# Weight halves interleaved element by element: a stationary operand read at a step of 8 bytes

## The chip, the cores and the metric

The kernel runs on one core of a Trainium2 chip. The metric is the device time of one execution in microseconds (us), first instruction to last and the little that lies around it; lower is better.

## What is computed

One inference step of a two-layer diffusion trunk for 128 context tokens and 512 latent tokens, D = 1024. Each layer is a mixer followed by a convolutional feed-forward block of width 2816. Layer 0's mixer is a bidirectional state-space scan beside a gated convolution, layer 1's is neighbourhood attention. Cut to the products with the large weights, which take nearly all of the time:

```python
u = h @ P['ssd_w_in'][e]                                  # layer 0: 1024 -> 5664 columns
... = jnp.concatenate([y_a, y_b], -1) @ P['mix0_w_out'][e]  # 2048 -> 1024
q, k, v = split(h @ P['na_w_qkv'][o])                     # layer 1: 1024 -> 3072
... = y @ P['na_w_out'][o]                                # 1024 -> 1024
g = dwconv(h @ P['ffn_w_gate'][i], P['ffn_conv_w'][i])    # both layers: 1024 -> 2816
u = h @ P['ffn_w_up'][i]
return (jax.nn.gelu(g) * u) @ P['ffn_w_down'][i]          # 2816 -> 1024
```

The scale, shift and gate vectors come from `silu(c) @ ada_w[i]` with 6 x 1024 columns a layer. All is float32, and the outputs are the two token blocks, the scan states and the context keys and values.

## The kernel before

The activations lie transposed: features on the 128 partitions, 642 columns (128 context tokens, 2 columns of padding, 512 latent tokens) on the free axis. Every large product is cut into 244 **slots**. A slot is a column block of a weight matrix, 128 output features wide and up to 1024 input features deep: [128 partitions, 8 x 128 elements]. Every product is made in three parts for precision: the weight and the activation are each split into a rounded high part and a low rest (type float32r), and the kernel sums high x high, high weight x low activation, and low weight x high activation.

A slot goes through four engines:

- **SyncE** (`weights`, the DMA at line 366) loads the slot into one of two `raw` buffers (RAW = 2). Before it issues the load it waits until GpSimd has finished with the slot two before (`low_split`). SyncE issues everything in order, so what is queued behind a weight load waits with it. In the mixer stage that includes a 1 MB load of `ada_w` (`ada_load`, line 422) after each of the steps of a head pair.
- **ScalarE** (`split`, line 1127) copies `raw` into the high part `w_hi`, once TensorE has used the slot four before (`slot_used`; RING = 4).
- **GpSimd** (`low`, line 560) writes the low part, `w_lo = raw - w_hi`, and counts `low_split`.
- **TensorE** (`half_slot`, lines 614 to 632) waits for `low_split` and makes for each of the 8 (in the down projection 6 or 5) blocks of 128 input features six matmuls: for both halves of the columns (322 and 320) the high part with the high (line 625) and with the low activation (line 626), then the low part with the high activation for both halves (line 629). Each of the six loads its stationary operand, 128 x 128, anew. That makes 10752 matmuls of 244 slots.

`w_hi` and `w_lo` are two buffers of [128, 4, 1024] elements, each contiguous in a partition. Nothing else reads or writes them, save at the start: `first5`, one of six buffers for the first columns of `ada_w`, lies over slots 2 and 3 of `w_lo` until the low parts need the place.

VectorE and ScalarE do the rest (scaling, convolution, gelu, residuals, norms) from PSUM. `ada_step` (line 696) is the TensorE work on a loaded piece of `ada_w`; there are four in each of the 8 head pairs, and one `ada` buffer.

Of the kernel before, what the change touches and what calls it, by code (L numbers as in the profile page):

```python
# [17 lines left out]
F32 = mybir.dt.float32  # L18
F32R = mybir.dt.float32r
# [4 lines left out]
P = 128  # L24
D = 1024
C = D // P
# [26 lines left out]
RAW, RING = 2, 4  # L53
# [9 lines left out]
ADA_N = 512  # L63
# [68 lines left out]
def trunk(nc, x_prompt, x_sample, state_ssd, cache_k, cache_v, c, c_ctx, ada_w, ada_b, norm_mix_g, norm_ffn_g,  # L132
# [6 lines left out]
    with ExitStack() as ctx:  # L139
        def sb(name, shape, dt=F32):  # L140
            return ctx.enter_context(nc.sbuf_tensor(name, shape, dt))
# [3 lines left out]


        raw = sb("raw", [P, RAW, C * P])
        w_hi = sb("w_hi", [P, RING, C * P], F32R)
        first_lo_at = -(-nc.sbuf_base // 32) * 32
        w_lo = sb("w_lo", [P, RING, C * P], F32R)  # L150
        assert nc.sbuf_base == first_lo_at + RING * C * P * 4, (nc.sbuf_base, first_lo_at)
        act_hi = sb("act_hi", [P, C * T], F32R)
        outs_at = -(-nc.sbuf_base // 32) * 32
        act_lo = sb("act_lo", [P, C * T], F32R)
# [26 lines left out]
        def at(name, off, shape, dt=F32):  # L181

            n = 4
            for s in shape[1:]:
                n *= s
            assert off + n <= arena_bytes, (name, off + n, arena_bytes)
            return nc.alloc_sbuf_tensor_at(name, shape, dt, offset=at_base + off)
# [27 lines left out]
        first_at = [2 * CT, AFTER + 4 * ROW, AFTER + 4 * ROW + 8192, AFTER + 4 * ROW + 16384,  # L215
                    (arena_bytes - 2 * D * 4) // 32 * 32]
        first = [at(f"first{n}", o, [P, 4, ADA_N]) for n, o in enumerate(first_at)]
        first += [nc.alloc_sbuf_tensor_at("first5", [P, 4, ADA_N], F32, offset=first_lo_at + 2 * C * P * 4)]
        quarters = [f[:, 2 * q:2 * q + 2, :] for f in first for q in range(2)]


# [2002 lines left out]
```

## Time and profile before

| | us |
|---|---|
| median of 3 runs | 1928.59 |
| range of the runs | 1928.18 to 1929.63 |
| span of the profiled execution | 1928.4 |
| TensorE matmul busy | 1878.8 |
| TensorE weight load busy | 1797.8 |
| VectorE / ScalarE / GpSimd busy | 1025.6 / 670.9 / 637.5 |

A row of the page or of a grouping view reads: line, engine, operation, output tile <- input tiles, shape, xcount, then busy time and mean duration in ns, then the idle time of the engine before these instructions and what ended it. PE is TensorE's matmuls, PEld its loads of stationary operands, DVE VectorE, ACT ScalarE, POOL GpSimd, SPq SyncE's queue. Matmuls are pipelined: a matmul row lasts some 310 ns, though the next starts much sooner. A timeline row gives start in us, duration in us, and the instruction.

### The profile page before, as it was taken

How to read it: one execution, taken by the hardware profiler on the slowest of the kernel's cores; microseconds unless marked ns; L12 is line 12 of the kernel's file. 1: busy time of each engine (PE TensorE's matmuls, PEld its weight loads, DVE VectorE, ACT ScalarE, POOL GpSimd, SP SyncE). 2: the span in 40 equal slices, each digit the busy share in tenths (PEclk: the TensorE clock that was granted, in tenths of full speed). 3: DMA queues.
4: the chain of work that ended last, by engine and by line, in shares of the span. 5: the costliest groups of instructions: out<-in, count | busy, mean ns of one | idle time of the engine just before them, and what ended most of it. 6: DMA issues, size and time to landing. Idle time of an engine off the chain costs nothing.

```text
span 1928.4 us, 35126 instructions
## 1 busy us (share of the span) xinstructions
PE 1878.8 (97%) x13424; PEld 1797.8 (93%) x13424; DVE 1025.6 (53%) x1927; ACT 670.9 (35%) x1022; POOL 637.5 (33%) x309
## 2 busy tenths in 40 slices
PE   5999999999999999999999999999999999999997
PEld 3998888888899999999999999987899999999997
DVE  5747788877614655314554353557566553145543
ACT  4443333232413443312334321157444433123332
POOL 1223222222232323443335433433133234433341
PEclk9999999999999999999999999999999999999998
DMA  8334545445442222222222433211312222222122
GB/s 307 95 84 157 164 141 170 153 155 169 156 151 77 77 76 71 66 82 76 76 59 62 152 92 88 82 46 30 104 57 77 76 70 67 82 77 76 55 67 75
DMA packets 276232, 192.49 MB, mean 100 GB/s; under 512 B 25515, under 2 KB 259367, under 8 KB 275639
## 3 DMA queue, kind: packets, MB, share of 16 engines
q1 hardware_dynamic: 270982, 182.78, 31.1%
q10 hardware_dynamic: 5168, 8.58, 1.3%
q8 instruction: 57, 0.93, 0.2%
q14 instruction: 25, 0.20, 0.0%
HBM read 181.29 MB, written 10.04 MB: 99 GB/s over the span
## 4 chain that ended last, share of the span: by engine, by line
PE 89%; issue 5%; DVE 2%; ACT 2%; POOL 1%; DMA 1%; SPq 0%; POOLq 0%; ACTq 0%; DVEq 0%
PE ps L625 26%; PE ps L626 26%; PE ps L629 25%; PE ps L696 2%; POOL w_lo L560 1%; PE ps L1074 1%; PE ps L888 1%; PE ps L1054 1%; PE ps L1020 1%; DVE act_lo L1643 1%; ACT sp L1436 1%; PE ps L720 1%; PE ps L1093 0%; PE ps L873 0%; PE ps L808 0%
## 5 line engine op out<-in xcount | busy, mean ns | idle before, releaser
L560 POOL TENSOR_TENSOR w_lo<-raw,w_hi 128x1024 fp32r<-128x1024 f32 x244 | 601.4, 2467 | 1203.3 <-ACT w_hi L1127 1197.2
L625 PE MATMUL ps<-act_hi,w_hi 128*128 128x322 f32 x2752 | 847.5, 315 | 3.7 <-DVE act_lo L1643 2.2
L626 PE MATMUL ps<-act_lo,w_hi 128*128 128x322 f32 x2624 | 799.7, 312 | 0.0
L629 PE MATMUL ps<-act_hi,w_lo 128*128 128x322 f32 x2752 | 631.8, 311 | 0.0
L625 PEld LDWEIGHTS ps<-act_hi,w_hi 128*128 128x128 f32 x2752 | 522.0, 190 | 17.0 <-issue 13.7
L626 PEld LDWEIGHTS ps<-act_lo,w_hi 128*128 128x128 f32 x2624 | 497.7, 190 | 0.0
L629 PEld LDWEIGHTS ps<-act_hi,w_lo 128*128 128x128 f32 x2752 | 466.1, 189 | 0.0
L1127 ACT ACTIVATE w_hi<-raw 128x1024 fp32r<-128x1024 f32 x244 | 256.2, 1051 | 361.5 <-PE ps L629 321.9
L625 PE MATMUL ps<-f_hi,w_hi 128*128 128x322 f32 x704 | 213.6, 311 | 0.0
L626 PE MATMUL ps<-f_lo,w_hi 128*128 128x322 f32 x704 | 212.9, 310 | 0.0
L1958 DVE SCALAR_TENSOR_TENSOR x<-ps,mod,x 128x128 f32 (+1 forms) x96 | 48.4, 546 | 270.0 <-PE ps L629 269.4
L629 PE MATMUL ps<-f_hi,w_lo 128*128 128x322 f32 x704 | 161.0, 310 | 0.0
L626 PEld LDWEIGHTS ps<-f_lo,w_hi 128*128 128x128 f32 x704 | 133.0, 189 | 0.0
L625 PEld LDWEIGHTS ps<-f_hi,w_hi 128*128 128x128 f32 x704 | 132.9, 189 | 0.0
L1727 DVE SCALAR_TENSOR_TENSOR ft<-fg,par,ft 128x642 f32<-128x642 f32 x44 | 123.9, 2816 | 6.8 <-DVE ft L1726 6.5
L629 PEld LDWEIGHTS ps<-f_hi,w_lo 128*128 128x128 f32 x704 | 118.5, 189 | 0.0
L1995 DVE TENSOR_TENSOR fg<-ps,spread 128x642 f32<-128x642 f32 x44 | 36.3, 826 | 132.2 <-PE ps L629 122.0
L1392 ACT ACTIVATE fe<-ft,gb 128x129 f32<-128x129 f32 x88 | 44.9, 558 | 126.9 <-DVE ft L1727 126.9
L1388 ACT ACTIVATE ft<-fg,par 128x642 f32<-128x642 f32 x44 | 36.7, 834 | 127.0 <-DVE fg L1995 126.9
L1545 DVE TENSOR_TENSOR acc<-acc,sq 128x642 f32<-128x642 f32 x40 | 60.3, 1509 | 25.2 <-ACT sq L1138 25.2
L1726 DVE SCALAR_TENSOR_TENSOR ft<-fg,par,ft 128x642 f32<-128x642 f32 x44 | 43.2, 983 | 44.0 <-ACT ft L1388 43.5
L1396 ACT ACTIVATE f_hi<-fa 128x642 f32 x44 | 32.6, 742 | 94.9 <-DVE fa L2007 94.9
(297 smaller groups left out, 1932.0 us busy)
## 6 DMA issues: line engine op xcount, KB each, us to landing
ada<-in_ada_w SPq DMA_DIRECT2D x40, 1024.0 KB, 6.1
raw<-in_ssd_w_in SPq DMA_DIRECT2D x44, 512.0 KB, 4.0
raw<-in_ffn_w_gate SPq DMA_DIRECT2D x44, 512.0 KB, 3.8
raw<-in_ffn_w_up SPq DMA_DIRECT2D x44, 512.0 KB, 3.8
raw<-in_ffn_w_down SPq DMA_DIRECT2D x32, 384.0 KB, 3.4
raw<-in_na_w_qkv SPq DMA_DIRECT2D x24, 512.0 KB, 3.8
raw<-in_ffn_w_down SPq DMA_DIRECT2D x32, 320.0 KB, 3.2
first<-in_ada_w SPq DMA_DIRECT2D x16, 512.0 KB, 10.2
```

Source lines behind the costliest of these rows:

```text
L560: g.tensor_tensor(w_lo[:, s], raw[:, s % RAW], w_hi[:, s], ALU.subtract).then_inc(S["low_split"], 1)
L625: t.matmul(out, hi, chunk_of(src_hi, k0 + k, cols), start=start, stop=False)
L626: t.matmul(out, hi, chunk_of(src_lo, k0 + k, cols), start=False, stop=False)
L629: mm = t.matmul(half_out(2 * tset, h), lo, chunk_of(src_hi, k0 + k, cols), start=False, stop=stop)
L696: mm = t.matmul(ps[g:g + ADA_COLS, bank, :], csil_w[:, 2 * q + k, :], ada[:, k, b * ADA_N:b * ADA_N + ADA_N], start=(q == 0), stop=(q == A ...
L1127: a(w_hi[:, s], raw[:, s % RAW], ACT.Copy).then_inc(S["high_split"], 1)
L1388: a(ft[k][:], fg[k][:, 1:T + 1], ACT.Copy, scale=w1).then_inc(S["ffn_mid"], 1)
L1392: ins = a(fe[k][:, lo:hi], ft[k][:, lo:hi], ACT.Gelu_apprx_tanh, bias=gb[:, k, stream:stream + 1])
L1545: tt(acc[:], acc[:], sq[:], ALU.add).then_inc(S["squares_used"], 1)
L1726: st.then_wait(stt(dst[:], buf[:, 0:T], w[:, bass.ds(w0, 1)], dst[:], ALU.mult, ALU.add))
L1727: return stt(dst[:], buf[:, 2:T + 2], w[:, bass.ds(w2, 1)], dst[:], ALU.mult, ALU.add)
L1958: ins = stt(dst, V(k)[:, lo:hi], gate, dst, ALU.mult, ALU.add)
```

## The change

The two buffers become one, `w_parts` of [128, 4, 1024, 2] elements. `w_hi` is its elements 0, 2, 4, ... and `w_lo` its elements 1, 3, 5, ... in each slot. The total size is the same. ScalarE now writes `w_hi` at a step of 8 bytes. GpSimd reads `w_hi` and writes `w_lo` at a step of 8 bytes, and still reads `raw` contiguously. TensorE loads all its stationary operands in `half_slot` at a step of 8 bytes, 128 elements over 1024 bytes of a partition instead of 512. The moving operands, the PSUM outputs, the DMAs, all waits and the order of instructions stay.

`first5` moves to slot 3 of the new buffer, so it lies over both parts of slot 3 and no longer over the low parts of slots 2 and 3.

```diff
         raw = sb("raw", [P, RAW, C * P])
-        w_hi = sb("w_hi", [P, RING, C * P], F32R)
-        first_lo_at = -(-nc.sbuf_base // 32) * 32
-        w_lo = sb("w_lo", [P, RING, C * P], F32R)
-        assert nc.sbuf_base == first_lo_at + RING * C * P * 4, (nc.sbuf_base, first_lo_at)
+        w_at = -(-nc.sbuf_base // 32) * 32
+        w_parts = sb("w_parts", [P, RING, C * P, 2], F32R)
+        w_hi, w_lo = w_parts[:, :, :, 0], w_parts[:, :, :, 1]
+        assert nc.sbuf_base == w_at + RING * C * P * 8, (nc.sbuf_base, w_at)
...
-        first += [nc.alloc_sbuf_tensor_at("first5", [P, 4, ADA_N], F32, offset=first_lo_at + 2 * C * P * 4)]
+        first += [nc.alloc_sbuf_tensor_at("first5", [P, 4, ADA_N], F32, offset=w_at + (RING - 1) * C * P * 8)]
```

## Rows read from the trace of the kernel before

**Rows 1.** The page: span, and busy time of the engines with their instructions.

```profile
span 1928.4 us, 35126 instructions
PE 1878.8 (97%) x13424; PEld 1797.8 (93%) x13424; DVE 1025.6 (53%) x1927; ACT 670.9 (35%) x1022; POOL 637.5 (33%) x309
```

**Rows 2.** The page: the chain that ended last, by engine and by line.

```profile
PE 89%; issue 5%; DVE 2%; ACT 2%; POOL 1%; DMA 1%; SPq 0%; POOLq 0%; ACTq 0%; DVEq 0%
PE ps L625 26%; PE ps L626 26%; PE ps L629 25%; PE ps L696 2%; POOL w_lo L560 1%; PE ps L1074 1%; PE ps L888 1%; PE ps L1054 1%; PE ps L1020 1%; DVE act_lo L1643 1%; ACT sp L1436 1%; PE ps L720 1%; PE ps L1093 0%; PE ps L873 0%; PE ps L808 0%
```

**Rows 3.** Stretches: span, busy PE, PEld, DVE, ACT, POOL, clock, DMA share, GB/s.

```profile
32.00:36.00 4.00, 3.55 (x16) 2.74 (x20) 3.04 (x6) 2.98 (x6) 0.00 (x0) 0.50 1.07 368
38.00:40.00 2.00, 2.00 (x22) 1.38 (x15) 1.24 (x2) 1.61 (x2) 0.31 (x1) 1.00 0.44 124
800.00:1000.00 200.00, 200.00 (x1352) 200.00 (x1352) 71.92 (x93) 53.65 (x65) 75.03 (x32) 1.00 0.26 76
```

**Rows 4.** Matmuls in order of time near 34 us, wide (128-column) stationary operands.

```profile
34.03 0.47 PE L625 MATMUL ps<-act_hi,w_hi 128*128 128x322 f32 x1
34.30 0.47 PE L626 MATMUL ps<-act_lo,w_hi 128*128 128x322 f32 x1
```

**Rows 5.** The same near 39 us: 32-column operands (L752, L753), then 128-column ones.

```profile
39.02 0.31 PE L752 MATMUL ps<-act_hi,wdt_hi 128*32 128x320 f32 x1
39.16 0.31 PE L753 MATMUL ps<-act_lo,wdt_hi 128*32 128x320 f32 x1
39.46 0.31 PE L625 MATMUL ps<-act_hi,w_hi 128*128 128x322 f32 x1
39.61 0.30 PE L626 MATMUL ps<-act_lo,w_hi 128*128 128x322 f32 x1
```

**Rows 6.** Loads of 32 and of 128 columns: durations in ns, minimum, median, maximum.

```profile
L752 PEld LDWEIGHTS ps<-act_hi,wdt_hi x16: 106/108/169, 32.4 to 53.4; 128*32 128x32 f32 x16
L856 PEld LDWEIGHTS ps<-xdw,btok x48: 187/192/192, 162.1 to 455.6; 128*128 128x128 f32 x48
L625 PEld LDWEIGHTS ps<-act_hi,w_hi x2752: 186/188/334, 33.8 to 1837.2; 128*128 128x128 f32 x197
```

**Rows 7.** Six matmuls with few moving columns, merged, and the duration of one.

```profile
330.19 0.83 PE L856 MATMUL ps<-xdw,btok 128*128 128x128 f32 x6
L856 PE MATMUL ps<-xdw,btok x48: 270/275/275, 162.2 to 455.7; 128*128 128x128 f32 x48
```

**Rows 8.** The two splitting operations, grouped, and GpSimd's durations.

```profile
L560 POOL TENSOR_TENSOR w_lo<-raw,w_hi 128x1024 fp32r<-128x1024 f32 x244 | 601.4, 2467 | 1203.3 <-ACT w_hi L1127 1197.2
L1127 ACT ACTIVATE w_hi<-raw 128x1024 fp32r<-128x1024 f32 x244 | 256.2, 1051 | 361.5 <-PE ps L629 321.9
L560 POOL TENSOR_TENSOR w_lo<-raw,w_hi x244: 2343/2397/3685, 27.9 to 1895.2; 128x1024 fp32r<-128x1024 f32 x122
```

**Rows 9.** GpSimd on an access pattern in short runs, grouped.

```profile
L589 POOL TENSOR_TENSOR bias<-win,masks 128x256 f32<-128x256 f32 x48 | 33.4, 730 | 55.9 <-DVE nmax L2103 55.9
```

**Rows 10.** One slot's low part and the first matmul on it, in order of time.

```profile
1031.39 2.54 POOL L560 TENSOR_TENSOR w_lo<-raw,w_hi 128x1024 fp32r<-128x1024 f32 x1 [5.03 <-ACT w_hi L1127]
1039.78 0.31 PE L625 MATMUL ps<-f_hi,w_hi 128*128 128x322 f32 x1
```

**Rows 11.** A head pair: low part, weight load, ada load, and ada's use.

```profile
243.90 2.41 POOL L560 TENSOR_TENSOR w_lo<-raw,w_hi 128x1024 fp32r<-128x1024 f32 x1 [9.12 <-ACT w_hi L1127]
246.47 0.37 SPq L366 DMA_DIRECT2D raw<-in_ssd_w_in  x1
247.09 0.38 SPq L422 DMA_DIRECT2D ada<-in_ada_w  x1
254.28 1.06 PE L696 MATMUL ps<-ada,csil_w 128*32 128x512 f32 x8
ada<-in_ada_w SPq DMA_DIRECT2D x40, 1024.0 KB, 6.1
```

**Rows 12.** A VectorE operation with two SBUF inputs that runs beside GpSimd's.

```profile
L1727 DVE SCALAR_TENSOR_TENSOR ft<-fg,par,ft 128x642 f32<-128x642 f32 x44 | 123.9, 2816 | 6.8 <-DVE ft L1726 6.5
```

## What the change does to the time: a prediction

> **What bounds the kernel now.** The first view is the page. TensorE's matmuls are busy 1878.8 of 1928.4 us, so it sits idle for 49.6 us in all; the other engines are busy about half the span or less [rows 1]. The chain that ended last agrees: 89% of it is TensorE, and 77% are the three lines of `half_slot` [rows 2]. A busy matmul row says little about pace, because rows overlap. So the second view counts: in the 200 us from 800 to 1000, all feed-forward matmuls, 1352 start [rows 3]. That is 200 / 1352 = 148 ns from one start to the next. The change touches the stationary operand of 10752 of these, and every nanosecond on that spacing is 10.8 us. What sets the spacing is therefore the question.
>
> Three things could: the moving columns, the load of the stationary operand, or a wait. Rows 4 and 5 separate them. Near 34 us the granted clock is 0.50, the 1.2 GHz level, and the spacing is 0.27 us, which is 322 columns at 1.2 GHz (268 ns) [rows 3, 4]. Near 39 us the clock is 1.00, and with 128-column operands the spacing is 0.15 us (39.46 to 39.61) [rows 3, 5]. The matmuls just before them, with stationary operands of only 32 columns, are spaced 0.14 us (39.02 to 39.16) [rows 5]. Loading a quarter of the columns buys next to nothing, so the moving side sets the pace (322 columns at 2.4 GHz are 134 ns, and about 14 ns come on top that do not depend on the load). The loads run beside.
>
> How far beside: a load of 32 columns takes 108 ns, one of 128 takes 188 to 192 [rows 6]. That is (190 - 108) / 96 = 0.85 ns a column, so 128 columns stream in 109 ns and some 80 ns are latency. Where moving columns are few, the loads set the pace, and it shows: six matmuls with 128 moving columns take 0.83 us, less one duration of 0.275 that is 0.555 for five spacings, 111 ns each [rows 7]. So contiguous loads need 111 ns a matmul and have 148. They can grow by a third, 37 ns or 0.29 ns a column, before the time moves at all. Beyond that it moves one for one.
>
> **The change part by part.** Nothing is added, removed or reordered. Three instructions get another access pattern.
>
> *The stationary loads* (10752 on lines 625, 626, 629). No row shows a load at a step of 8 bytes. From above, a load spans twice the bytes, so I bound it by twice the streaming: 111 becomes 222 ns, the spacing 222, and 74 ns x 10752 = 796 us. From below it is nothing: no gain is possible, since even a quarter of the columns did not shorten the spacing. I take nothing, and choose it by a rate. The moving operand is read contiguously at 2.4 GHz: 322 columns of 4 bytes in 148 ns are 8.7 bytes a ns and partition, 9.6 inside its 134 ns. The stationary operand reads an element every 0.85 ns, and at a step of 8 bytes it passes over 9.4 bytes a ns. If memory hands out whole pieces of 8 or 16 bytes, the new load asks for no more pieces a ns than the moving operand already gets [rows 3, 6]. The cover is the 37 ns; without it each nanosecond of load costs 10.8 us.
>
> The Trainium skill has two statements on this, and they differ. "SBUF — State Buffer" (Door 1, the note on cachelines) says that SBUF delivers at full rate if each 16-byte line is hit at least twice; at 8 bytes a step each line is hit exactly twice, and the sum would be zero. "Vector Engine (DVE) Microarchitecture Reference" (section 5.2, the access granule) says that a VectorE port needs pairs of adjacent words, and that hopping with every element raised 1.054 to 1.73 ns a column. No run here shows either.
>
> *ScalarE's write of `w_hi`* (244 x 1051 ns) and *GpSimd's `w_lo`* (244 x 2467 ns) [rows 8]. Neither is busy enough to bind: GpSimd sat 1203 us waiting, 1197 of them for the high part, and the high part waited 322 us for TensorE to free a slot [rows 8]. A slot lasts 48 x 148 ns = 7.1 us; the two operations in series take 3.5. Bounds: ScalarE between 0 and a doubling, +1.05 us. GpSimd's nearest row with a broken pattern is 730 ns for 256 elements, 2.85 ns each against 2.41, so +0.45 us for 1024 [rows 8, 9]; its longest instance now, 3685 ns, sets the far end, +1.2 us. Call the sum of both e: 0 to 2.3 us, and I take 0.5, the GpSimd row alone. Below 0 I exclude: half as many adjacent elements cannot be quicker to write.
>
> What hides e is the ring. TensorE starts a slot well after its low part is ready: 1031.39 + 2.54 = 1033.93 against 1039.78, a slack of 5.9 us, the smallest I found once the first slots are through [rows 10]. The thinner cover is SyncE's queue. In a head pair the low part that ends at 246.31 releases a weight load at 246.47, and the ada load behind it goes at 247.09. It lands after 6.1 us at 253.2, and TensorE uses it at 254.28 [rows 11]. So e is free up to 1.1 us there; above it TensorE waits. The pattern stands seven times, once in each head pair but the first. At the start of the kernel, before the ring is full, nothing hides e: I count it once, +0.5 us, less than 2.3 at worst.
>
> *VectorE.* Its operation on line 1727 takes 2816 ns, though the same operation one line above it on the same shape is far shorter, because GpSimd's instruction runs beside it [rows 12]. A longer GpSimd instruction lengthens it by up to the same amount, 44 times. VectorE is busy 72 of 200 us there [rows 3], so I cost it at nothing; in the mixer it would join the ada case.
>
> *`first5`*: its waits stay, and the first split of slot 3 comes long after TensorE has read it. Nothing.
>
> **The sum.** Span 1928.4 + 0 (loads) + 0.5 (start) + 0 (ring) = 1928.9, with 0.2 around the span (median 1928.59) 1929.1, say 1929 us.
>
> **The rivals.**
>
> *The load outgrows its cover (slower).* It decides from a load streaming 1.33 times as long. Twice as long gives 1928.6 + 796 = 2725 us; 1.5 times gives a spacing of about 167, +19 ns x 10752 = +204, 2133 us. For it: a 4-byte element out of every 8 is a different pattern from every long read in the trace. Against it: the rate above, and that loads run at 0.85 ns a column while moving columns run at 0.42, so there is time. I give 0.13. By VectorE's factor in the Trainium skill ("Vector Engine (DVE) Microarchitecture Reference", section 5.2), 1.73 / 1.054 = 1.64, the estimate would be 111 x 1.64 = 182 ns, +34 x 10752 = +366 us, 2295 us.
>
> *The splits outgrow SyncE's slack (slower).* It decides from e = 1.1 us. At e = 2.3 TensorE waits 1.2 us for one ada load in each of seven pairs, for two if the next is as tight: 8 to 17 us, and 2.3 at the start, together 1939 to 1948 us. For it: the slack is thin. Against it: both operations must come near their far bounds. I give 0.09.
>
> *Something gets quicker.* TensorE has 49.6 us of idle time, but nothing in the change reaches it except a shorter split, which I exclude above. A gain would need a conflict between readers of the two buffers that the trace does not name: one tenth of the 14 ns on top of the moving columns would be 15 us, 1914 us. I give 0.04.
>
> The forecast keeps 0.74. That the change does nothing at all gives the same time, and only the durations of the loads and splits can tell it apart.
>
> **How the numbers follow.** A measurement of this kernel can tell 0.2%, 3.9 us. Same: 0.74. Slower: 0.13 + 0.09 = 0.22. Faster: 0.04. The range takes in the forecast with its bounds (e from 0 to 1.1) and the whole second rival: 1926 to 1949. It leaves out the load rival (0.13) and the gain (0.04), 0.17 in all; the load's time, once over the cover, has no natural place to stop.
>
> **What would show it right or wrong.** Right: matmul starts in 800 to 1000 still number about 1352, and a matmul load stays near 188 ns. If the load is longer but below some 225 ns (188 + 37), the cover holds and the count stays. Wrong by the first rival: the load row is above that, the count falls (1100 at 182 ns, 900 at 222), and the spacing is equal at lines 625, 626 and 629, which all changed, while L752's is not. Wrong by the second: the groups of L560 and L1127 sum to over 4.6 us instead of 3.5, and line 696 shows idle time before it, released by the ada DMA. The step I am least sure of is the memory's price for a step of 8 bytes.

## The result, and the profile after

The changed kernel takes 1942.68 us (median of 4 runs, 1939.81 to 1943.73) against 1929.11 us before (4 runs, 1928.18 to 1930.66): 1.0067 times as long, 95% interval 1.0055 to 1.0079. That is 13.6 us more. The time lies inside the predicted range, but not where the likeliest case had it: this is slower by more than 0.2%, which had a chance of 0.22.

The page of the changed kernel, its span, busy times and chain, to be laid beside [rows 1, 2]:

```profile
span 1942.0 us, 35126 instructions
PE 1891.5 (97%) x13424; PEld 1811.1 (93%) x13424; DVE 1039.2 (54%) x1927; ACT 694.5 (36%) x1022; POOL 644.4 (33%) x309
PE 89%; issue 5%; DVE 2%; ACT 2%; POOL 1%; DMA 1%; SPq 0%; POOLq 0%; ACTq 0%; DVEq 0%
```

TensorE is still nearly all of the chain. Its busy time grew by 12.7 us, and its idle time (span less busy) went only from 49.6 to 50.5. So TensorE did not wait more; it went slower while busy. The stretches show where. Columns as in [rows 3]:

```profile
84.00:88.00 4.00, 4.00 (x18) 4.00 (x19) 3.13 (x4) 1.81 (x2) 0.50 (x1) 0.50 0.50 131
88.00:92.00 4.00, 4.00 (x17) 4.00 (x16) 3.09 (x4) 0.50 (x2) 2.41 (x1) 0.50 0.05 9
800.00:1000.00 200.00, 200.00 (x1342) 200.00 (x1341) 70.07 (x88) 55.98 (x64) 78.00 (x32) 1.00 0.26 76
```

From 800 to 1000 there are 1342 starts where there were 1352 [rows 3], at a clock of 1.00 in both: 149.0 ns a matmul instead of 147.9. The same over the whole kernel, worked out from all starts that follow within 165 ns (some 10,500): 149.29 against 148.19 ns. The difference, 1.1 ns, over the 10656 steps from one such matmul to the next inside the large products is 11.7 us of the 13.6. The granted clock has little part in the rest. It did fall at other times: through 88 to 92 us it stood at 0.50, where before it was back at 0.89,

```profile
84.00:88.00 4.00, 4.00 (x18) 4.00 (x19) 2.51 (x5) 2.19 (x4) 0.89 (x1) 0.50 0.47 131
88.00:92.00 4.00, 4.00 (x26) 4.00 (x26) 3.70 (x16) 0.00 (x0) 1.48 (x1) 0.89 0.25 61
```

which are nine matmuls, 1.3 us. (These two lines are of the kernel before.) But elsewhere it went the other way: from 470 to 510 us it was 0.96 where it had been 0.91, from 1430 to 1470 us 1.00 for 0.96, and from 610 to 650 us 0.91 for 0.96. Over the whole execution the mean is 0.990, before 0.989.

The instructions that the change touches, of the changed kernel, durations in ns as minimum, median, maximum; their counterparts are [rows 6, 8]:

```profile
L625 PEld LDWEIGHTS ps<-act_hi,w_parts x2752: 193/196/334, 34.0 to 1850.0; 128*128 128x128 f32 x197
L629 PEld LDWEIGHTS ps<-act_hi,w_parts x2752: 192/196/334, 35.0 to 1850.4; 128*128 128x128 f32 x197
L1127 ACT ACTIVATE w_parts<-raw x244: 1122/1148/1196, 26.9 to 1907.5; 128x1024 fp32r<-128x1024 f32 x122
L560 POOL TENSOR_TENSOR w_parts<-raw,w_parts x244: 2380/2440/3625, 28.1 to 1908.7; 128x1024 fp32r<-128x1024 f32 x122
```

A load takes 196 ns instead of 188, ScalarE's split 1148 instead of 1047, GpSimd's 2440 instead of 2397. And line 696, where a late ada load would show:

```profile
250.11 0.38 SPq L422 DMA_DIRECT2D ada<-in_ada_w  x1
...
257.36 1.07 PE L696 MATMUL ps<-ada,csil_w 128*32 128x512 f32 x8
```

The first tight load goes at 250.11 and TensorE uses it at 257.36, 7.25 us later; before it was 7.19 [rows 11]. No new wait arose there.

### The profile page after: what moved, and what is told of

Read it like the earlier page. It is cut to its first block, busy times and chain, and to the rows that moved or that the text cites. A ratio compares the mean times of both kernels' runs of the same rounds, so it can differ in the third digit from the quotient of the medians.

```text
span 1942.0 us, 35126 instructions
## 1 busy us (share of the span) xinstructions
PE 1891.5 (97%) x13424; PEld 1811.1 (93%) x13424; DVE 1039.2 (54%) x1927; ACT 694.5 (36%) x1022; POOL 644.4 (33%) x309
## 4 chain that ended last, share of the span: by engine, by line
PE 89%; issue 5%; DVE 2%; ACT 2%; POOL 1%; DMA 1%; SPq 0%; POOLq 0%; ACTq 0%; DVEq 0%
PE ps L625 26%; PE ps L629 26%; PE ps L626 25%; PE ps L696 2%; POOL w_parts L560 1%; PE ps L1074 1%; PE ps L888 1%; PE ps L1054 1%; PE ps L1020 1%; DVE act_lo L1643 1%; ACT sp L1436 1%; PE ps L720 0%; PE ps L1093 0%; PE ps L873 0%; PE ps L808 0%
## 5 line engine op out<-in xcount | busy, mean ns | idle before, releaser
L560 POOL TENSOR_TENSOR w_parts<-raw,w_parts 128x1024 fp32r<-128x1024 f32 x244 | 608.2, 2495 | 1210.0 <-ACT w_parts L1127 1203.9
L625 PE MATMUL ps<-act_hi,w_parts 128*128 128x322 f32 x2752 | 850.9, 316 | 4.3 <-DVE act_lo L1643 2.2
L626 PE MATMUL ps<-act_lo,w_parts 128*128 128x322 f32 x2624 | 802.0, 312 | 0.0
L629 PE MATMUL ps<-act_hi,w_parts 128*128 128x322 f32 x2752 | 638.0, 314 | 0.0
L625 PEld LDWEIGHTS ps<-act_hi,w_parts 128*128 128x128 f32 x2752 | 543.2, 197 | 17.5 <-issue 14.2
L626 PEld LDWEIGHTS ps<-act_lo,w_parts 128*128 128x128 f32 x2624 | 516.7, 197 | 0.0
L629 PEld LDWEIGHTS ps<-act_hi,w_parts 128*128 128x128 f32 x2752 | 476.7, 197 | 0.0
L1127 ACT ACTIVATE w_parts<-raw 128x1024 fp32r<-128x1024 f32 x244 | 280.1, 1149 | 357.9 <-PE ps L629 317.6
L625 PE MATMUL ps<-f_hi,w_parts 128*128 128x322 f32 x704 | 215.8, 313 | 0.0
L626 PE MATMUL ps<-f_lo,w_parts 128*128 128x322 f32 x704 | 214.6, 312 | 0.0
L629 PE MATMUL ps<-f_hi,w_parts 128*128 128x322 f32 x704 | 162.4, 312 | 0.0
L625 PEld LDWEIGHTS ps<-f_hi,w_parts 128*128 128x128 f32 x704 | 137.8, 196 | 0.0
L626 PEld LDWEIGHTS ps<-f_lo,w_parts 128*128 128x128 f32 x704 | 137.8, 196 | 0.0
L1727 DVE SCALAR_TENSOR_TENSOR ft<-fg,par,ft 128x642 f32<-128x642 f32 x44 | 129.8, 2951 | 6.8 <-DVE ft L1726 6.5
L629 PEld LDWEIGHTS ps<-f_hi,w_parts 128*128 128x128 f32 x704 | 121.3, 196 | 0.0
```

The costliest lines, as they stand in the source:

```text
L560: g.tensor_tensor(w_lo[:, s], raw[:, s % RAW], w_hi[:, s], ALU.subtract).then_inc(S["low_split"], 1)
L625: t.matmul(out, hi, chunk_of(src_hi, k0 + k, cols), start=start, stop=False)
L626: t.matmul(out, hi, chunk_of(src_lo, k0 + k, cols), start=False, stop=False)
L629: mm = t.matmul(half_out(2 * tset, h), lo, chunk_of(src_hi, k0 + k, cols), start=False, stop=stop)
L1127: a(w_hi[:, s], raw[:, s % RAW], ACT.Copy).then_inc(S["high_split"], 1)
L1727: return stt(dst[:], buf[:, 2:T + 2], w[:, bass.ds(w2, 1)], dst[:], ALU.mult, ALU.add)
```

## The experiments

The theories. **A**: a load of a stationary operand at a step of 8 bytes makes each matmul 1.1 ns longer, though the load is some 30 ns short of being the bound. **B**: the strided writes of ScalarE and GpSimd disturb TensorE's reads. **C**: the place of the weights relative to the activations matters, and any new place could cost or give as much. Each kernel is compared with the kernel before, run on the same chip: median 1930.27 us (21 runs) beside the blocks, the strided writes, the strided loads and the step of 16 bytes, 1929.40 (25 runs) beside the same place, the high or low loads and the 12 bytes, 1930.22 (13 runs) beside the last four. A ratio is that of the two kernels' runs, with its 95% interval.

### Both parts contiguous in one buffer

```diff
-        w_parts = sb("w_parts", [P, RING, C * P, 2], F32R)
-        w_hi, w_lo = w_parts[:, :, :, 0], w_parts[:, :, :, 1]
+        w_parts = sb("w_parts", [P, RING, 2, C * P], F32R)
+        w_hi, w_lo = w_parts[:, :, 0], w_parts[:, :, 1]
```

> One buffer as in the changed kernel, but each slot holds the high part in one contiguous piece and the low part behind it; nothing is read or written at a step. In the traces the spacing of matmul starts in the stretch from 800 to 1000 us went from 148 ns (1352 starts) to 149 ns (1342), and 1.1 ns x 10752 is 12 of the 13.6 us lost. Theory A, the step of the load costs it: here 1929 us, within 2 us of the kernel before, 1352 starts. Theory B, the strided writes of ScalarE and GpSimd disturb TensorE's reads: 1929 us as well. Theory C, it is only where the parts lie relative to the activations: the low parts have moved here too, so the time may lie anywhere from 1920 to 1945 us.

Measured: 1929.61 us, ratio 0.9999 (0.9990 to 1.0008); load 188 ns. One buffer, with `first5` moved, costs nothing.

### Strided writes, contiguous loads

```diff
-                    hi, lo = w_hi[:, s, k * P:k * P + P], w_lo[:, s, k * P:k * P + P]
+                    hi, lo = w_flat[:, s, k * P:k * P + P], w_flat[:, s, (C + k) * P:(C + k) * P + P]
```

(`w_flat` is the slot as 2048 elements in a row; the writes are those of the changed kernel.)

> ScalarE and GpSimd write and read the two parts at a step of 8 bytes as in the changed kernel; TensorE loads contiguously, from the first and the second half of the slot, so its stationary operands are the wrong elements (the large products are changed by that, the amount of work is not). Theory A (step of the load): 1929 to 1931 us, 1352 starts in the stretch, load 188 ns, while ScalarE's split keeps its 1149 ns and GpSimd's its 2495 ns. Theory B (strided writes): 1942 us and 1342 starts. Theory C (place): the same time as the kernel with contiguous blocks, whatever that is.

Measured: 1931.92 us, ratio 1.0007 (0.9998 to 1.0016). The stretch and the two splits:

```profile
800.00:1000.00 200.00, 200.00 (x1352) 200.00 (x1352) 70.27 (x88) 55.65 (x64) 78.84 (x33) 1.00 0.26 76
L1128 ACT ACTIVATE w_parts<-raw 128x1024 fp32r<-128x1024 f32 x244 | 278.3, 1142 | 352.6 <-PE ps L630 312.3 <-DMA raw<-in_ffn_w_gate 13.6 <-DMA raw<-in_na_w_out 10.6
L561 POOL TENSOR_TENSOR w_parts<-raw,w_parts 128x1024 fp32r<-128x1024 f32 x244 | 608.2, 2495 | 1203.8 <-ACT w_parts L1128 1197.7 <-DVE qt L2118 6.0
```

The splits are as long as in the changed kernel, and TensorE keeps its 1352 starts. Theory B falls. What the slower splits themselves cost is 1.3 us by the ratio, with an interval that takes in zero. The profiled execution, the longest of the 11, shows one place where they can cost something. Line 697 (696 in the kernel before) waits 3.3 us for the ada load, once, in the first head pair; the kernel before waits 1.3 us there, the changed kernel 1.4, the other kernels with contiguous writes 0.9 to 1.5:

```profile
PE ps L697 <- DMA ada<-in_ada_w: 3.3, 1, 3.3
```

### Contiguous writes, strided loads

```diff
-                g.tensor_tensor(w_lo[:, s], raw[:, s % RAW], w_hi[:, s], ALU.subtract).then_inc(S["low_split"], 1)
+                g.tensor_tensor(w_flat[:, s, C * P:2 * C * P], raw[:, s % RAW], w_flat[:, s, 0:C * P], ALU.subtract).then_inc(S["low_split"], 1)
...
-                a(w_hi[:, s], raw[:, s % RAW], ACT.Copy).then_inc(S["high_split"], 1)
+                a(w_flat[:, s, 0:C * P], raw[:, s % RAW], ACT.Copy).then_inc(S["high_split"], 1)
```

> The other half alone: ScalarE and GpSimd write the two parts as contiguous blocks of a slot; TensorE loads at a step of 8 bytes over the slot, so its stationary operands are the wrong elements (the large products are changed by that, the amount of work is not). Theory A: 1941 to 1943 us, 1342 starts, load 196 ns, ScalarE's split back at 1051 ns. Theory B: 1929 us, 1352 starts, though the load still takes 196 ns. Theory C: any time, but not that of the kernel with contiguous blocks, since the loads start at other places.

Measured: 1939.41 us, ratio 1.0050 (1.0037 to 1.0064).

```profile
800.00:1000.00 200.00, 200.00 (x1342) 200.00 (x1341) 69.27 (x88) 51.87 (x63) 76.11 (x32) 1.00 0.26 76
```

The 1342 starts are back, with ScalarE's split at 1051 ns, and the spacing over the whole kernel is 149.29 ns, as in the changed kernel. The loads alone make 9.7 us by the ratio (7 to 12), a little under the 11.7 of the spacing and under the 1941 us that was expected. The granted clock accounts for most of the gap: these runs have a mean clock of 0.990 to 0.993, those of the kernel before 0.989 to 0.991. Runs at 0.990 alone are 1940.8 us here (2 runs), 1931.5 with strided writes (4) and 1929.5 before (12): 11.3 us for the loads and 2.0 us for the writes, together 13.3 of the 13.6. These are few runs, and why the clock differs between the kernels stays open.

### The same place without a step

```diff
-        w_parts = sb("w_parts", [P, RING, C * P, 2], F32R)
+        w_parts = sb("w_parts", [P, RING, C, 2, P], F32R)
...
-                    hi, lo = w_hi[:, s, k * P:k * P + P], w_lo[:, s, k * P:k * P + P]
+                    hi, lo = w_hi[:, s, k], w_lo[:, s, k]
```

> Every block of 128 x 128 keeps the 1024 bytes of a partition that it has in the changed kernel, but the high part is the first 512 of them and the low part the other 512, each contiguous. So the loads start at the places of the changed kernel (within 512 bytes) and have no step. With two blocks per slot the time was 1929.6 us; with strided loads 1939.4. Theory A, the step costs the 1.1 ns a matmul: 1929 to 1930 us, 1352 starts from 800 to 1000 us, load 188 ns. Theory C, the place costs it: 1940 us and 1342 starts, with a load of 188 ns.

Measured: 1928.83 us, ratio 1.0000 (0.9991 to 1.0009), load 188 ns, spacing 148.18 ns over all starts. Three contiguous layouts (two buffers, two blocks a slot, two blocks for each 128 features) give 148.18 to 148.19 ns. Theory C falls for the places tried; theory A stands.

### High or low loads alone

The writes are contiguous blocks. The first line of the diff strides the high parts only, the second, in a kernel of its own, the low parts only.

```diff
+                    hi, lo = w_hi[:, s, k * P:k * P + P], w_flat[:, s, (C + k) * P:(C + k) * P + P]
...
+                    hi, lo = w_flat[:, s, k * P:k * P + P], w_lo[:, s, k * P:k * P + P]
```

> Parts written as contiguous blocks; only the high part's four loads of six go at a step of 8 bytes, the low part's two are contiguous (the high part's elements are the wrong ones, which changes the large products and not the amount of work). Theory A with an equal cost for each load: two thirds of the 10 us of all strided loads, 1936 us, load 196 ns at lines 625 and 626 and 188 at 629. Theory D, only some hand-overs between loads and moving operands pay: in the changed kernel the spacing from the fourth matmul of six to the fifth, under which a low part's load runs, did not change (148.3 to 148.0 ns), the others rose by 0.6 to 2.4 ns; then this kernel has nearly the whole cost, 1937 to 1939 us.

> The counterpart: only the low part's two loads of six at a step of 8 bytes, the high part's contiguous (wrong elements in the low part only; the amount of work is the same). Theory A with an equal cost for each load: 1933 us, load 188 ns at lines 625 and 626 and 196 at 629. Theory D: 1930 to 1932 us.

Measured: 1933.61 us (ratio 1.0025, 1.0015 to 1.0036) with the four high loads strided, 1928.76 us (ratio 1.0004, 0.9994 to 1.0013) with the two low ones. Both are below what either theory gave, and the second is not told apart from the kernel before by its time. Here too the clock was the higher one, up to 0.992; in runs at 0.991 alone the three kernels take 1934.6 (3 runs), 1929.8 (2) and 1928.2 us (2 before), which is 6.3 and 1.6 us. The spacing does not need such a choice. The loads of the first kernel:

```profile
L625 PEld LDWEIGHTS ps<-act_hi,w_parts x2752: 192/196/334, 34.7 to 1840.3; 128*128 128x128 f32 x197
L629 PEld LDWEIGHTS ps<-act_hi,w_parts x2752: 187/188/334, 35.8 to 1840.8; 128*128 128x128 f32 x197
```

Spacing in ns from each of the six matmuls to the next, worked out from the starts:

```
                      1->2   2->3   3->4   4->5   5->6   6->1   mean
contiguous            149.2  148.3  148.0  148.3  148.2  147.2  148.19
low loads strided     148.7  148.6  148.2  147.1  149.4  148.4  148.41
high loads strided    150.3  148.3  149.2  149.2  147.8  148.0  148.78
all loads strided     149.8  149.5  149.2  147.9  149.9  149.4  149.29
```

(The first row is the kernel before, the last the kernel with strided loads alone.)

The cost grows with the number of strided loads, +0.22, +0.59 and +1.10 ns, somewhat more than in proportion for all six. Theory D had put nearly all of it on the high loads; the low ones have less of it than their share, but the two kernels together make 0.8 of 1.1, so neither equal shares nor theory D is right. Over 10656 steps they are 2.3, 6.3 and 11.7 us. The rows of the table rise and fall by more than the means, so a single place among the six proves little.

### Steps of 16 and of 12 bytes

The writes are contiguous blocks again; the first two lines are the kernel at 16 bytes, the last the one at 12.

```diff
+                    at = k // 4 * 4 * P + k % 4
+                    hi, lo = (w_flat[:, s, o + at:o + at + 4 * (P - 1) + 1:4] for o in (0, C * P))
...
+                    hi, lo = (w_flat[:, s, o + k // 3 * 3 * P + k % 3:o + k // 3 * 3 * P + k % 3 + 3 * P - 2:3] for o in (0, 7 * P))
```

> As the kernel with strided loads alone, but with the loads at a step of 16 bytes inside each contiguous part (128 elements over 2048 bytes; the large products are changed by that, the amount of work is not). The load went from 188 to 196 ns at 8 bytes. Theory A in its linear form, 8 ns of load and 1.1 ns of spacing for every doubling or for every 8 bytes: load 204 to 212 ns, spacing 150 to 151 ns, 1953 to 1965 us. If each element now costs an access of its own and the load passes its cover of 37 ns: load above 230 ns, spacing 150 to 222 ns, above 1960 us and up to 2725 us. Theory B: 1929 us. Theory C: anywhere from 1920 to 1945 us.

> All loads at a step of 12 bytes (the wrong elements of the slot, the same amount of work). A load took 188, 196 and 332 ns at steps of 4, 8 and 16 bytes. If what counts is how many elements a piece of 16 bytes gives (4, 2, 1, here 4 elements from 3 pieces): two of four elements come in pairs at full rate and two alone, so halfway between 8 and 16 bytes: load 264 ns, streaming 184 ns, spacing near 170, about 2160 us. If the cost follows the bytes passed over with a threshold above 8: load near 332 ns and 2850 us, or near 204 ns and 1950 us.

Measured: 2849.04 us (ratio 1.476, 1.474 to 1.479) at 16 bytes and 2221.07 us (ratio 1.151, 1.149 to 1.154; 2 runs) at 12. The stretch and a load at 16 bytes:

```profile
800.00:1000.00 200.00, 200.00 (x868) 198.01 (x867) 67.53 (x104) 51.75 (x73) 41.34 (x18) 1.00 0.17 50
L627 PEld LDWEIGHTS ps<-act_hi,w_parts x2752: 307/332/336, 35.2 to 2715.3; 128*128 128x128 f32 x197
```

and at 12 bytes:

```profile
800.00:1000.00 200.00, 200.00 (x1135) 200.00 (x1135) 54.03 (x70) 51.63 (x58) 66.20 (x29) 1.00 0.22 63
L625 PEld LDWEIGHTS ps<-act_hi,w_parts x2752: 250/265/334, 34.7 to 2116.9; 128*128 128x128 f32 x197
```

At 16 bytes TensorE makes 868 starts in this stretch, 230 ns each on average; from one matmul of the large products to the next the median is 235 ns. The load is the bound. This is the first rival of the prediction, at twice the step it was made for, and it went past the far end of what was expected, 222 ns and 2725 us: one element for each 16 bytes costs more than twice the contiguous pace. The 12-byte load came out at 264 ns in the median over all its lines (265 on this one), where counting elements per 16 bytes gave 264: of four elements two share a piece and two are alone. The spacing that was expected with it, 170 ns and 2160 us, was too low; it is 176 ns.

The same loads in the few us in which the granted clock is at 0.50 (the 1.2 GHz level) tell something else. Here is the kernel at 16 bytes, first the stretch, then its loads near 36 us, then its matmuls:

```profile
35.40:36.40 1.00, 1.00 (x5) 1.00 (x5) 1.00 (x2) 0.98 (x2) 0.00 (x0) 0.50 1.15 324
L627 PEld LDWEIGHTS ps<-act_hi,w_parts x2: 332/333/334, 35.2 to 35.7; 128*128 128x128 f32 x2
35.43 0.47 PE L627 MATMUL ps<-act_hi,w_parts 128*128 128x322 f32 x1
35.70 0.47 PE L628 MATMUL ps<-act_lo,w_parts 128*128 128x322 f32 x1
```

The spacing is 0.27 us, as in [rows 4], and a load takes 333 ns, as it does at this clock in the kernel before (334, median). So at the lower clock a step of 16 bytes costs nothing here; at the higher one it costs 87 ns a matmul, and the load itself is no quicker than at the lower.

### The load's own pace, contiguous and at 8 bytes

```diff
-                        mm = t.matmul(half_out(2 * tset, h), lo, chunk_of(src_hi, k0 + k, cols), start=False, stop=stop)
+                        mm = t.matmul(half_out(2 * tset, h)[:, 0:64], lo, chunk_of(src_hi, k0 + k, slice(cols.start, cols.start + 64)), start=False, stop=stop)
```

> Measures the load's own pace, contiguous. As the kernel with blocks in the same place, but the low part's two matmuls of six read only 64 of their 322 or 320 moving columns (work is left out there: most of the low weight's share of the products), so that the load of the next stationary operand sets the spacing from the fifth matmul of six to the sixth. Expected from the prediction's load-bound rows: 111 ns there, 148 ns at the others; about 1800 us.

> The same narrow matmuls (the same work left out) on the changed kernel, all parts at a step of 8 bytes. The load lasts 8 ns longer there. Theory P: the step leaves the pace of loads alone and adds latency only; spacing from the fifth to the sixth matmul 111 to 113 ns, and the cover of 37 ns stands. Theory Q: the 8 ns are pace; spacing 119 ns. Theory R: loads at 8 bytes already run near the cover (that is why each matmul lost 1.1 ns); spacing 140 to 148 ns.

Measured: 1827.5 and 1853.9 us (2 runs each). The same 200 us, contiguous and then at 8 bytes:

```profile
760.00:960.00 200.00, 200.00 (x1475) 200.00 (x1473) 80.03 (x102) 59.14 (x72) 83.88 (x36) 1.00 0.28 81
```

```profile
760.00:960.00 200.00, 200.00 (x1444) 200.00 (x1443) 79.95 (x98) 61.28 (x71) 83.90 (x35) 1.00 0.28 80
```

Six matmuls take 814 ns in the first and 831 in the second. I had expected to see the load's pace from the fifth matmul to the sixth; that one is 30 ns, since the sixth's load was already under way, and the pace shows one place later. It is read best from the starts of the loads themselves, where one load follows the other without room. Three loads of each kernel, contiguous and then at 8 bytes:

```profile
801.08 0.19 PEld L625 LDWEIGHTS ps<-f_hi,w_parts 128*128 128x128 f32 x1
801.19 0.19 PEld L626 LDWEIGHTS ps<-f_lo,w_parts 128*128 128x128 f32 x1
801.34 0.19 PEld L625 LDWEIGHTS ps<-f_hi,w_parts 128*128 128x128 f32 x1
```

```profile
800.92 0.20 PEld L625 LDWEIGHTS ps<-f_hi,w_parts 128*128 128x128 f32 x1
801.04 0.20 PEld L626 LDWEIGHTS ps<-f_lo,w_parts 128*128 128x128 f32 x1
801.19 0.20 PEld L625 LDWEIGHTS ps<-f_hi,w_parts 128*128 128x128 f32 x1
```

Over all slots the median from the sixth load to the first of the next six is 109 ns contiguous and 117 ns at 8 bytes (1696 cases), and from that one to the second 111 and 118 ns (1792 cases). So the 8 ns of a longer load are 7 to 8 ns of pace: theory Q (119), near enough, and neither P (111 to 113) nor R. The starts of the matmuls say the same when both places are taken: from the sixth to the first and on to the second they are 109 + 231 ns contiguous and 115 + 239 ns at 8 bytes, 14 ns more for two loads. The cover at 8 bytes is 148 - 118 = 30 ns, not gone. The expected 1800 us for the contiguous kernel was 27 us too low.

### A slower split

```diff
-                a(w_hi[:, s], raw[:, s % RAW], ACT.Copy).then_inc(S["high_split"], 1)
+                [a(w_hi[:, s, q:q + 64], raw[:, s % RAW, q:q + 64], ACT.Copy) for q in range(0, C * P, 64)][-1].then_inc(S["high_split"], 1)
```

> Prices the second rival of the prediction on the kernel before, all else unchanged: ScalarE makes each high part in 16 pieces of 64 elements, so the split is expected to last about 4 us instead of 1.05, e = 3 us. By the prediction's reading (a slack of 1.1 us before an ada load, one or two such loads in each of seven pairs, and e once at the start): 7 x 1.9 to 14 x 1.9 + 3 = 16 to 30 us, 1945 to 1960 us, with idle time before line 696 released by the ada DMA. If the ring covers it all: 1929 to 1932 us. If ScalarE's own other work is delayed and that binds first: over 1960 us.

Measured: 1946.52 us, ratio 1.0092 (1.0075 to 1.0109), 16 us more. In a head pair:

```profile
253.70 2.38 POOL L560 TENSOR_TENSOR w_lo<-raw,w_hi 128x1024 fp32r<-128x1024 f32 x1 [9.50 <-ACT w_hi L1127]
256.24 0.37 SPq L366 DMA_DIRECT2D raw<-in_ssd_w_in  x1
256.86 0.38 SPq L422 DMA_DIRECT2D ada<-in_ada_w  x1
263.06 1.07 PE L696 MATMUL ps<-ada,csil_w 128*32 128x512 f32 x8 [0.65 <-DMA ada<-in_ada_w]
L696 PE MATMUL ps<-ada,csil_w 128*32 128x512 f32 x320 | 42.6, 605 | 8.9 <-DMA ada<-in_ada_w 8.9
```

From the ada load to its use are 6.20 us where there were 7.19 [rows 11]: the slack is gone, and line 696 has idle time, 8.9 us in nine waits where the kernel before has 1.3 us in one. The pieces overlap, so from the start of the first to the end of the sixteenth are 2.44 us (median) and not 4, and e was 1.4 us. For that e the working of the second rival gives 0.3 us for each of 7 to 14 ada loads and 1.4 us at the start, 3.5 to 5.6 us. The loss is three times as much or more. It fell within what was expected for e = 3 by chance.

Seven of the nine waits are the prediction's, one in each head pair but the first; they sum to 4.6 us, 0.66 us each. The other two lie in the first pair, which the prediction had left out, though the kernel before already has its 1.3 us there. TensorE's waits from 130 to 180 us:

```profile
PE ps L696 <- DMA ada<-in_ada_w: 4.3, 2, 2.7
PE ps L808 <- DVE mbuf L1852: 2.2, 1, 2.2
```

The second use of `ada` came at 168.74 us, in the kernel before at 160.91, so 7.8 us were lost before the first pair was over; a wait of 1.4 us for ScalarE at line 769, near 55 us, and about 1 us of lower clock (0.95 from 40 to 60 us, before 1.00) are in it. Over the whole kernel the ada loads make 7.6 of the 16 us (8.9 less 1.3). Most of the rest are waits for ScalarE and VectorE that the second rival does not have.

### Moving operands at a multiple of 64 bytes

```diff
+        def even_chunk(buf, k, cols):
+            at = (k * T + 15) // 16 * 16 if cols.start == 0 else (k * T + cols.start) // 16 * 16
+            return buf[:, at:at + cols.stop - cols.start]
```

> On the kernel before, the moving operands of the large products start at a multiple of 64 bytes instead of at 2568 x k or 2568 x k + 1288 bytes (each start is moved by up to 15 elements, which changes the products; the amount of work is the same). In the traces the spacing of matmuls is the same to 1 ns in every slot for a given place among the 48 and differs between places, from 141 to 157 ns, where 322 columns need 134. Theory: how the moving operand lies to the pieces of memory makes part of the 14 ns; then 137 to 145 ns and 1815 to 1900 us. Rival: it does not matter; 148 ns and 1929 us.

Measured: 1926.85 us, ratio 0.9980 (0.9971 to 0.9990).

```profile
800.00:1000.00 200.00, 200.00 (x1353) 200.00 (x1352) 72.87 (x93) 53.65 (x65) 75.86 (x32) 1.00 0.26 75
```

One start more in 200 us. The expected 137 to 145 ns did not come; the rival was nearly right. Single places moved by up to 2.7 ns in the mean (the fourth to the fifth from 148.3 to 145.6, the second to the third from 148.3 to 150.8), the mean by 0.25. Alignment of the moving operand, counted from the start of its buffer, redistributes the 14 ns and does not remove them.

No version here beats the kernel before by more than this 0.2%, and this one reads other elements; the layout with contiguous parts is the one to keep.

## Why the prediction came out as it did, step by step

- **What bounds the kernel: right.** TensorE's spacing carries 11.7 of the 13.6 us, and its idle time hardly moved.
- **The moving side sets the spacing, the load runs beside with 37 ns to spare: right as a bound.** Measured on its own the contiguous load's pace is 109 to 111 ns (111 from [rows 7]), and a load of 264 or 332 ns puts the time well above. The sign of 225 ns (188 + 37) takes the duration of a load for its pace: by it loads of 264 and 332 ns would give 148 + 39 = 187 and 148 + 107 = 255 ns; measured were 176 and 235. The duration outside the pace is not fixed: 188 - 110 = 78 ns contiguous, 88 and 97 at 12 and 16 bytes.
- **"They can grow by a third ... before the time moves at all": wrong, and this is the step that failed.** The load grew by 8 ns, a fifth of the cover, and every matmul by 1.1. The prediction took the spacing for the larger of two numbers. The runs show a leak: of 8 ns under cover, 14% comes through, with strided loads alone as with the whole change, and in none of three contiguous layouts. Over 10752 instructions that made 0.6%. I had a row that could have warned me: 322 columns need 134 ns and take 148, so something beyond the larger of the two was already in the spacing, and I left it unexplained because it did not depend on the load's width.
- **The price of a step of 8 bytes: taken as nothing, measured as 7 to 8 ns of pace in 110, 8 ns of duration.** The choice by rate (whole pieces of 8 or 16 bytes, no more of them a ns than the moving operand gets) pointed the right way: at 8 bytes a load takes 7% longer by its pace, at 16 bytes 2.1 times as long. The Trainium skill's cacheline rule ("SBUF — State Buffer", Door 1) is what the runs at 12 and 16 bytes show for TensorE's loads; "full rate" at two hits a line is short by the 7%. VectorE's rule of adjacent pairs ("Vector Engine (DVE) Microarchitecture Reference", section 5.2) would have made the load 1.64 times as long at 8 bytes; measured 1.07, so it does not hold for this port.
- **ScalarE and GpSimd: e = 0.5 taken, 0.14 measured** (101 and 43 ns by the medians). The split of the two was wrong: I gave it all to GpSimd, and ScalarE has more than half. Below 1.1 us it was to cost nothing in the pairs, and in the changed kernel it did cost nothing there (line 696 waits 1.4 us in all, before 1.3).
- **VectorE: costed at nothing, and nothing came of it.** Its operation on line 1727 went from 2816 to 2951 ns (means), more than the 43 ns of GpSimd's instruction beside it: GpSimd's instruction also starts 101 ns later against it (67 ns before it, where it was 168, medians), which is what ScalarE's split grew by. TensorE's idle time did not follow. In the kernel with the slow split, where all but 2 of its 44 instances have no splitting operation of GpSimd beside them, it takes 980 ns: the neighbour is what made it long, as [rows 12] was read.
- **The start: 0.5 us.** The run with strided writes leaves 1.3 us for all effects of the splits, 2.0 at equal clock, few runs in the second case. The slow split shows that the start can cost several times e, so counting e once was too little as a rule, though e was small here. The first head pair, which the prediction excepts from the ada waits, is where such a wait stands already in the kernel before. The sum's other small term, 0.2 us around the span, sets a median beside the span of another execution; in every run that has both on record a time is 1.7 us longer than its span. The forecast is the median before plus 0.5 either way.
- **The rivals.** The load rival is right in kind and needs a step of more than 8 bytes. The split rival did not occur; its late ada load is real, but its sum gives a third, at most, of what a slower split cost. The time fell into the range by luck, because the range was stretched for the split rival; the true cause was none of the cases, and lay between the forecast and the load rival.
- **The signs to look for** served: the count in the 200 us fell with the load at 196 ns, which the text had said it would not below 225.

What stays open: why a covered load lengthens the matmul beside it, what the 14 ns on top of the 134 are, and 1.9 us of the 13.6, about what the strided writes cost at equal clock. One fact narrows the first two. At the lower clock the matmuls of both kernels are spaced 267 ns (medians of 45 and 51 cases), the 268 that 322 columns need: there neither the 14 ns nor the 1.1 ns exist.

## What to carry to other kernels

A stationary operand may be read at a step of 8 bytes without falling off a cliff, but not for free, and at 12 or 16 bytes the cliff is there: keep it contiguous where the layout is free to choose, as here. "Hidden" work beside a saturated engine is not worth nothing when there are ten thousand instructions: one per cent of one instruction's spacing is one per cent of the kernel, so before costing a covered change at zero, look whether the spacing already exceeds both of its bounds (it did here; that this is a sign in general is not shown). A layout change is best tried in halves, writes alone and reads alone, even where the result of each is not the product.

## What the runs showed of the hardware

Loads of a 128 x 128 float32r stationary operand, by step, at the higher clock; the pace is the time from the start of one load to that of the next where the loads bind. The elements are 4 bytes.

| step, bytes | load, ns (median) | pace, ns | spacing with 322 and 320 moving columns, ns |
|---|---|---|---|
| 4 | 188 | 109 to 111 | 148.2 |
| 8 | 196 | 117 to 118 | 149.3 |
| 12 | 264 | 176 | 176 |
| 16 | 332 | 235 | 235 |

At 12 and 16 bytes the loads bind in the kernel itself, and pace and spacing are the same number. A column costs 0.86, 0.92, 1.38 and 1.84 ns. The third is the mean of the second and the fourth, as it should be if two elements in one 16 bytes go at the full rate and a lone one at half of it.

At the lower clock a load takes 331 to 334 ns at each of the four steps and the matmuls are spaced 267 or 268 ns (medians of 29 to 55 cases), so there the step has no price.

ScalarE writes 1024 elements at a step of 8 bytes in 1142 to 1149 ns instead of 1051, 0.09 ns an element; GpSimd's subtraction with one input and the output at that step takes 1% more by the means (2495 for 2467 ns), 2% by the medians. In the consecutive slots of one product of the feed-forward block the spacing of matmuls is the same to about 1 ns for a given place among a slot's 48, and it differs between places by up to 16 ns (141 to 157); the place of the weights did not change it, the alignment of the moving operand and the step of the load did.
